# Three buffers instead of two for the gate and up weights of a mixture-of-experts stage, with the loads issued further ahead

## What is computed

```python
D_MODEL, D_EXPERT, N_EXPERTS, TOP_K = 1024, 512, 32, 2
# each token goes to the 2 best of the 8 experts in its best group of 4
def expert_mlp(args):
    xb, e = args
    h = jax.nn.silu(xb @ w_gate[e]) * (xb @ w_up[e])
    return h @ w_down[e]
# y[token] += gate * expert_mlp(x[token]); then x = LayerNorm(alpha*x + y)
```

## Time and profile before

| | |
|---|---|
| median of three runs | 2394.74 us |
| the profiled execution's own time | 2395.6 us |
| its span, first to last instruction | 2393.7 us |
| TensorE matmuls busy | 2159.0 us, 90% of the span |
| VectorE / ScalarE / GpSimd busy | 638.6 / 334.2 / 336.1 us |
| chain that ended last | 81% TensorE, 7% VectorE, 2% DMA |
| mean DMA rate | 220 GB/s |

### The profile page before, as it was taken

One profiled execution on the slowest core, in us unless ns is written; L12 is line 12 of the kernel. 1 busy time (PEld: TensorE's weight loads), 2 busy tenths in 40 slices (PEclk: granted clock), 3 DMA queues, 4 the chain that ended last, 5 costly groups with the idle time before them and its releaser, 6 DMA issues.

```text
span 2393.7 us, 29459 instructions
## 1 busy us (share of the span) xinstructions
PE 2159.0 (90%) x9808; PEld 1417.0 (59%) x9808; DVE 638.6 (27%) x1255; ACT 334.2 (14%) x827; POOL 336.1 (14%) x440
## 2 busy tenths in 40 slices
PE   7999978887999999999589999888699999999994
PEld 5566644555666666666356665444476666666662
DVE  1212166562111111111422113656601111111115
ACT  2000023210111111111010001323011111111111
POOL 0100011111111111111221000121111111111113
PEclk8999999997999999999789999999899999999995
DMA  7401011146899999999351110213459999999963
GB/s 246 125 32 39 18 48 72 53 167 229 313 381 387 372 374 373 376 373 356 134 186 36 36 36 19 65 72 121 180 217 348 373 378 380 368 377 375 368 247 147
DMA packets 101804, 526.37 MB, mean 220 GB/s; under 512 B 16362, under 2 KB 25578, under 8 KB 84994
## 3 DMA queue, kind: packets, MB, share of 16 engines
q1 hardware_dynamic: 86882, 491.58, 53.2%
q0 software_dynamic: 14848, 33.85, 5.6%
HBM read 489.95 MB, written 58.27 MB: 229 GB/s over the span
## 4 chain that ended last, share of the span: by engine, by line
PE 81%; DVE 7%; issue 5%; DMA 2%; POOL 2%; SPq 2%; ACT 1%; DVEq 0%; POOLq 0%; ACTq 0%
PE ps L775 21%; PE ps L544 19%; PE ps L808 11%; PE ps L660 9%; PE ps L779 8%; PE ps L812 4%; PE ps L758 3%; PE ps L612 1%; DVE arena L1545 1%; POOL rstd L1614 1%; DVE arena L1435 1%; PE ps L670 1%; DMA arena<-in_w_in 1%; DVE arena L1217 1%; DVE stat L1538 1%
## 5 line engine op out<-in xcount | busy, mean ns | idle before, releaser
L544 PE MATMUL ps<-arena 128*128 128x344 f32 x1728 | 510.7, 457 | 7.3 <-DMA arena<-in_w_in 4.5
L775 PE MATMUL ps<-arena 128*128 128x256 f32 x2304 | 510.0, 382 | 2.5 <-DVE arena L1435 2.5
L775 PEld LDWEIGHTS ps<-arena 128*128 128x128 f32 x2304 | 438.0, 191 | 87.6 <-issue 28.9
L544 PEld LDWEIGHTS ps<-arena 128*128 128x128 f32 x1728 | 331.1, 192 | 181.5 <-issue 14.4
L808 PE MATMUL ps<-arena 128*128 128x512 f32 x576 | 255.8, 597 | 20.3 <-ACT arena L1003 19.1
L1446 DVE SCALAR_TENSOR_TENSOR arena<-ps,gates,arena 128x256 f32<-128x256 f32 (+1 forms) x128 | 61.5, 480 | 664.2 <-ACT arena L998 664.2
L660 PE MATMUL ps<-arena 128*128 128x512 f32 x512 | 225.6, 598 | 14.3 <-ACT arena L951 11.0
L1658 POOL DMA_INDIRECT ytok<-arena,scol x64 | 98.7, 1542 | 973.1 <-DVE arena L1459 566.1
L781 PE MATMUL ps<-arena 128*64 128x256 f32 x896 | 199.4, 381 | 0.0
L779 PE MATMUL ps<-arena 128*64 128x256 f32 x896 | 199.4, 381 | 0.0
L808 PEld LDWEIGHTS ps<-arena 128*128 128x128 f32 x576 | 106.5, 190 | 148.3 <-issue 122.1
(11 more groups left out here) (217 smaller groups left out, 1695.1 us busy)
## 6 DMA issues: line engine op xcount, KB each, us to landing
arena<-in_w_gate SPq DMA_DIRECT2D x64, 2048.0 KB
arena<-in_w_up SPq DMA_DIRECT2D x64, 2048.0 KB, 19.9
arena<-in_w_down SPq DMA_DIRECT2D x64, 2048.0 KB, 20.0
arena<-in_w_in SPq DMA_DIRECT2D x36, 512.0 KB, 3.3
arena<-out_y_all SPq DMA_DIRECT2D x16, 512.0 KB, 3.2
xs<-arena SPq DMA_DIRECT2D x16, 512.0 KB, 2.7
ytok<-arena SPq DMA_DIRECT2D x16, 512.0 KB, 3.5
arena<-ytok SPq DMA_DIRECT2D x16, 512.0 KB, 6.5
```

Of the source, the lines that this page charges most:

```text
L544: last = mm(ps[:, 3 * half + ch, 0:CH], wring[:, slot, k * P:(k + 1) * P], xT[:, k, ch * CH:(ch + 1) * CH], start=(k == 0), stop=(k == KD ...
L775: last = mm(ps[:, 2 + q, at_c:at_c + 256], xgT[:, slot, k], w[slot][:, k, cols], start=(k == 0), stop=(k == KD - 1))
```

## The change

`wg` and `wu` get a third slot, at 32336 and 36432 of the arena. `wd`, `xgT` and `xg` keep two. Expert n uses slot n % 3 for gate and up weights, and n % 2 for down weights. TensorE raises `gu_mm` by 6 instead of 4 at the start, so the wait in `gate_up_in`, whose text is unchanged, is now for the expert three before; the waits of ScalarE and VectorE on `gu_mm` are moved by the same 2. Since 14 pairs don't divide by 3, TensorE's loop becomes 4 rounds of 3 pairs, with 2 of the 14 pairs and the last pair written out behind it. SyncE's loop becomes 4 rounds of 6 experts, between 2 experts ahead of it and 4 behind. SyncE also waits for the last output projection (`wo_mm`) before `order_ready`, since the third slot lies on `wo`.

```diff
+TURNS3 = ((NE + 2) // 3, (NE + 1) // 3, NE // 3)
...
-        wg = (at(8256, KD, DE), at(0, KD, DE))
-        wu = (at(12352, KD, DE), at(4096, KD, DE))
+        wg = (at(8256, KD, DE), at(0, KD, DE), at(32336, KD, DE))
+        wu = (at(12352, KD, DE), at(4096, KD, DE), at(36432, KD, DE))
...
-                def ranked_in(n, slot, col):
-                    e = sp.value_load(order[0:1, ds(col, 1)], min_val=0, max_val=NE - 1)
-                    gate_up_in(n, slot, e)
-                    down_in(n, slot, e)
-
+                def ranked_expert(col):
+                    return sp.value_load(order[0:1, ds(col, 1)], min_val=0, max_val=NE - 1)
+
+                sp.wait_ge(s["wo_mm"], BASE + NT * (l + 1) + 2)
+                settle(sp, s["sp_passed"])
                 sp.wait_ge(s["order_ready"], BASE + l + 1)
                 settle(sp, s["sp_passed"])
-                with sp.Fori(0, NPAIR) as i:
-                    ranked_in(2 * i + 2, 0, i + FIRST)
-                    ranked_in(2 * i + 3, 1, i + WIDE)
-                for slot in range(2):
-                    ranked_in(NE - 2 + slot, slot, WIDE - 2 + slot)
+                e = ranked_expert(FIRST)
+                gate_up_in(2, 2, e)
+                down_in(2, 0, e)
+                e = ranked_expert(WIDE)
+                gate_up_in(3, 0, e)
+                down_in(3, 1, e)
+                with sp.Fori(0, 4) as i:
+                    for j in range(6):
+                        e = ranked_expert(3 * i + (FIRST + 1 + j // 2 if j % 2 == 0 else WIDE + 1 + j // 2))
+                        gate_up_in(6 * i + 4 + j, (j + 1) % 3, e)
+                        down_in(6 * i + 4 + j, j % 2, e)
+                for j in range(4):
+                    n = NE - 4 + j
+                    e = ranked_expert((WIDE - 3, NE - 1, WIDE - 2, WIDE - 1)[j])
+                    gate_up_in(n, n % 3, e)
+                    down_in(n, j % 2, e)
...
-            pe.sem_inc(s["gu_mm"], 4)
+            pe.sem_inc(s["gu_mm"], 6)
...
-                    pe.wait_ge(s[f"wg_in{slot}"], BASE + 16 * (NE // 2 * l + turn + 1))
-                    pe.wait_ge(s[f"wu_in{slot}"], BASE + 16 * (NE // 2 * l + turn + 1))
+                    pe.wait_ge(s[f"wg_in{slot3}"], BASE + 16 * (TURNS3[slot3] * l + turn3 + 1))
+                    pe.wait_ge(s[f"wu_in{slot3}"], BASE + 16 * (TURNS3[slot3] * l + turn3 + 1))
...
-                with pe.Fori(0, NPAIR) as i:
-                    pair(2 * i + 2, i + 1, HALF, True)
-                pair(NE - 2, NE // 2 - 1, P, False)
+                with pe.Fori(0, NPAIR // 3) as i:
+                    for j in range(0, 6, 2):
+                        pair(6 * i + 2 + j, 3 * i + 1 + j // 2, ((j + 2) % 3, j % 3),
+                             (2 * i + (j + 2) // 3, 2 * i + (j + 3) // 3), HALF, True)
+                for j in range(0, 6, 2):
+                    e = NE - 6 + j
+                    pair(e, e // 2, (e % 3, (e + 1) % 3), (e // 3, (e + 1) // 3), HALF if j < 4 else P, j < 4)
...
-                    act.wait_ge(s["gu_mm"], BASE + 2 * n + 2)
+                    act.wait_ge(s["gu_mm"], BASE + 2 * n + 4)
```

More of the change, by code:

```diff
@@ L263, in build @@
             "ov_m", "ov_inv", "ov_idx",
-            "wg_in0", "wg_in1", "wu_in0", "wu_in1", "wd_in0", "wd_in1", "xg_in0", "xg_in1", "xg_mm",
+            "wg_in0", "wg_in1", "wg_in2", "wu_in0", "wu_in1", "wu_in2", "wd_in0", "wd_in1", "xg_in0", "xg_in1", "xg_mm",
             "xg_a", "xg_d", "gu_mm", "silu", "h_ready", "dn_mm", "y_a", "y_d", "sc_out0", "sc_out1", "ht_mm", "ht_a", "ht_d",
@@ L276, in build @@
                 "const_in", "copied", "ident_in", *(f"l2_in{t}" for t in range(NT)), "lnp_in", "ov_w", "small_out", "smp_in", "state_in", "w_in0",
-                "w_in1", "w_in2", "wd_in0", "wd_in1", "wg_in0", "wg_in1", "wo_in", "wu_in0", "wu_in1", "x1_out0",
+                "w_in1", "w_in2", "wd_in0", "wd_in1", "wg_in0", "wg_in1", "wg_in2", "wo_in", "wu_in0", "wu_in1", "wu_in2", "x1_out0",
                 "x1_out1", "x2_out", "xin0", "xin1", "xr_in0", "xr_in1"),
@@ L760, in gathered, with gate_up @@
                     last.then_inc(s["xg_mm"], 1)
-                def gate_up(e, slot, turn, rows):
+                def gate_up(e, slot, slot3, turn3, rows):
                     n = NE * l + e
@@ L774, in gate_up @@
                                 for k in range(KD):
-                                    last = mm(ps[:, 2 + q, at_c:at_c + 256], xgT[:, slot, k], w[slot][:, k, cols],
+                                    last = mm(ps[:, 2 + q, at_c:at_c + 256], xgT[:, slot, k], w[slot3][:, k, cols],
                                               start=(k == 0), stop=(k == KD - 1))
@@ L778, in gate_up @@
                             for k in range(KD):
-                                mm(ps[HALF:P, 2 + q, 0:256], xgT[:, slot, k, 0:HALF], wg[slot][:, k, cols],
+                                mm(ps[HALF:P, 2 + q, 0:256], xgT[:, slot, k, 0:HALF], wg[slot3][:, k, cols],
                                    start=(k == 0), stop=(k == KD - 1))
-                                last = mm(ps[0:HALF, 2 + q, 0:256], xgT[:, slot, k, 0:HALF], wu[slot][:, k, cols],
+                                last = mm(ps[0:HALF, 2 + q, 0:256], xgT[:, slot, k, 0:HALF], wu[slot3][:, k, cols],
                                           start=(k == 0), stop=(k == KD - 1))
@@ L816, in down, with pair @@
                     last.then_inc(s["dn_mm"], 1)
-                def pair(e, turn, second, then):
-                    gate_up(e, 0, turn, P)
+                def pair(e, turn, slot3, turn3, second, then):
+                    gate_up(e, 0, slot3[0], turn3[0], P)
                     gathered(e + 1, 1, turn, second)
@@ L822, in pair @@
                     down(e, 0, turn, P)
-                    gate_up(e + 1, 1, turn, second)
+                    gate_up(e + 1, 1, slot3[1], turn3[1], second)
                     if then:
@@ L829, in _ @@
                 gathered(0, 0, 0, P)
-                pair(0, 0, P, True)
+                pair(0, 0, (0, 1), (0, 0), P, True)
                 settle(pe, s["pe_passed"])
-                with pe.Fori(0, NPAIR) as i:
-                    pair(2 * i + 2, i + 1, HALF, True)
-                pair(NE - 2, NE // 2 - 1, P, False)
+                with pe.Fori(0, NPAIR // 3) as i:
[5 more added lines that the diff above has]
+                    pair(e, e // 2, (e % 3, (e + 1) % 3), (e // 3, (e + 1) // 3), HALF if j < 4 else P, j < 4)
                 settle(pe, s["pe_passed"])
@@ L994, in silu @@
                     for q in range(2):
-                        act.wait_ge(s["gu_mm"], BASE + 2 * n + q + 1 + 4)
+                        act.wait_ge(s["gu_mm"], BASE + 2 * n + q + 1 + 6)
                         act.wait_ge(s["h_ready"], BASE + 2 * n + q - 1)
@@ L1433, in xg_evict @@
                     dve.wait_ge(s["xg_mm"], BASE + n + 3)
-                    dve.wait_ge(s["gu_mm"], BASE + 2 * n + 2)
+                    dve.wait_ge(s["gu_mm"], BASE + 2 * n + 4)
                     v.tensor_copy(xgT[:, slot, 4:8, 0:rows], ps[:, 1, :].rearrange("p (k t) -> p k t", k=4)[:, :, 0:rows]
```

## The result

The changed kernel is slower: its runs gave 2408.15 to 2413.2 us, median 2412.35 (4 runs), against a median of 2394.3 of the kernel before in the same comparison. The ratio is 1.0073, with a 95% interval from 1.0056 to 1.0091. The forecast was 2402.0 us with a range up to 2412.0; the median lies 0.35 us above the end of that range, and the loss of 18 us is two and a half times the 7.3 us of the sum.

The account below looks back on a forecast made before the run. TensorE was taken as the bound, with the DMA queue close behind. Only the delayed first gathers cost time, 4.0 + 3.3 = 7.3 us, all other terms 0: 2402.0 us against the median of 2394.74, range up to 2412.

Parts of the forecast that it names:

- The steady loop: Loop of 14 pairs: the third slot removes no wait, since TensorE never waits for weights there; 0 us.
- theory G: Follow-up theory, not in the forecast: expert 2's 4 MiB load, issued just ahead of the first gather, slows that gather.
- the gather under load: Each layer's first gather, beside expert 2's early loads: 9.9 us instead of 5.94 and 6.58, adding 7.3 us; bound 12.7.
- other engines: Moved waits of ScalarE and VectorE are the same conditions, and SyncE's longer program delays nothing: 0 us.
- the length of TensorE's code: TensorE's loop body grows from one pair to three, 4.4 code packets instead of 1.5; taken as 0 us.
- Case A: Likeliest case: first gather of each layer delayed, all else hidden; 2402.0 us, own range 2395 to 2407.4; chance 57%.
- Rival C: TensorE's longer loop no longer stays resident, so each jump back needs a code fetch; some 2426 us; chance 15%.
- R: Follow-up theory, not in the forecast: a new register instruction lengthens the stretch before each full expert's down multiplication.
- The other sign: Second sign named for TensorE's loop code not staying resident: code packets in every round of the loop.
- Rival B: First gather of each layer lands as before, so the kernel is not slower: price 0, 2394.7 us; chance 22%.

Follow-up runs that it names:

- e6: Changed kernel with expert 2's gate and up loads issued after the first gather lands, and the down-weight wait behind the gate-and-up matmuls: 2394.08 us, ratio 1.0002.
- e1: Changed kernel, but SyncE issues expert 2's gate and up loads only after the layer's first gather has landed: 2403.94 us, ratio 1.0044.
- e9: Changed kernel, but only expert 2's gate weights (2 MiB) are issued before the first gather lands, the up weights after it: 2411.26 us, one execution.
- e7: Kernel before, with the waits for down weights and the last result's evictions moved out of down() to behind the gate-and-up matmuls: 2397.21 us, ratio 1.0017.
- e8: Kernel before, but all three loads of expert 1 are issued after the first gather has landed: 2392.5 us, ratio 0.9992.
- e10: Kernel before with expert 1's loads behind the first gather, and TensorE waiting for rk_done only behind the last expert: 2390.08 us, ratio 0.9981.
- e4: Kernel before, with only the down-weight semaphores and TensorE's waits on them 1 higher, so the value needs its own register instruction: 2401.83 us, ratio 1.0037.
- e5: Changed kernel, but the wait for the down weights stands behind the gate-and-up matmuls, before the transposes: 2405.45 us, ratio 1.0053.

## Why the prediction was right and wrong

**Right.** The steady loop gains nothing from the third slot: no weight wait was there, and e6 shows the slot by itself at 1.0002. The gate load of expert 2 is issued at 548.68 us, 0.16 us before the gather at 548.84, and the gather, named as the place of the loss, is where more than half of it lies. That is theory G, shown by e1. The issue and the first transposes (548.68 and 560.05 us, forecast about 552 and 563) came some 3 us early, since the stretch before them was shorter in this execution.

**A size was off: the gather under load.** The step took 9.9 us, the median of the gathers in the loop; it measured 10.97 and 11.41. The sum had 4.0 + 3.3 = 7.3 us for it, and it is 5.03 + 4.83 = 9.9, within the bound of 12.7. The prediction named a bias to the other side, that those 26 gathers run behind a scatter; why this one is slower still, no run tells.

**Not a term of the sum: the first gate-and-up.** It took 16.79 and 16.60 us in the two layers, instead of 16.10 and 15.76: 1.5 us more in all. Its length goes with the granted clock, which is the share of full speed: 0.50, its lower level, in the 9 us or so of waiting ahead of it, and 1.00 from 6 us behind its start. In its first 6 us it was 0.65 and 0.71 in the kernel before, 0.54 and 0.57 in the changed one. Behind gathers of 10 to 12 us it took 16.36 to 16.84 us in seven of eight cases (15.59 in e9), behind gathers of about 6 us 15.49 to 16.10 in eleven of twelve (17.01 in e7). But in e8 and e10, with the shortest gathers, it took 16.31 to 16.84 in all four. So the gather's length doesn't set it by itself, and whether the 1.5 us belong to the change stays open.

**The step that failed: "other engines" and the loop.** The prediction went through the moved waits of ScalarE and VectorE ("the same conditions: 0") and through the length of TensorE's code, but not through what the new wait values cost TensorE. It forecast the full gate-and-ups "still 36.22 us apart"; they are 36.46. The register instruction, and the waits that it pushes behind the end of the last eviction, cost 0.25 us per pair, and 32 pairs make it 8.0 us, which stood in the sum as 0. e4 shows it in the old kernel (7.1 us), and in e5 it is gone. The sum is now 9.9 + 8.0 = 17.9 us, against 18 between the medians (13 to 22 by the interval).

**What was luck.** That the measured time lies only 0.35 us above the range is not the sum's merit. Case A by itself ended at 2407.4; the range went up to 2412 as a margin for rivals of another kind, and the 8 us of the loop filled it.

**Rival C, the code that doesn't stay, fell,** and its sign was badly chosen: a period other than 36.22 us was to be C, and it was R. The other sign was right. In the changed kernel's DMA view from 722 to 1050 us, three rounds of the new loop with two of its three jumps back (827.8 and 937.2), there are two queues and none of them is code:

```profile
q1 hardware_dynamic: 14593, 112.86, 86.3%
q0 software_dynamic: 4032, 9.53, 11.4%
```

The 12 more code packets of the whole program (52 for 40) are fetched when the longer straight code is passed: 4 come from 612 to 722 us, the loop's first round among it, none from 722 to 1050 (nor from 716 to 724, around the first jump back at 718.4), and 7 from 1050 to 1170, where the loop is left. The kernel before has 4 from 603 to 1170. The Trainium skill's rule of a two-page window ("Runtime: NRT & Kernel Launch", Instruction fetch mechanics) would have a fetch at each jump of this loop, whose body is 4.4 packets long; the trace doesn't agree. The 128 KiB that the same section gives for TensorE are compatible with it: at 0.85 MB for 52 packets the body is, by estimate, some 72 KB.

**Rival B, the gather lands as before,** fell with the gathers themselves, 10.97 and 11.41 us.

## What to carry to other kernels

A prefetch that is issued earlier is not free even when it is early enough not to be waited for: look which small transfer on the critical path it now runs beside, and issue it behind that one. A change of buffer counts also changes the values that engines wait for; where a value was shared between semaphores, look at the instruction list for a new register instruction between an eviction and the matmul that waits for it, and move such a wait to where the engine has work queued. What costs is whatever stands behind the wait that ends last, here about 0.1 us for each instruction; waits that are long satisfied cost nothing ahead of it. Before adding a buffer, read whether anything waits for what it holds.

## What the runs showed that was not expected

One register instruction, with the wait that it pushes behind the last eviction's end, costs 0.25 us per use on TensorE, and nothing if it stands behind the gate-and-up matmuls (e5). No engine's busy time shows it. What stays open is why the compiler groups the waits as it does, and why the wait on `ht_d` alone (e7) ends 0.05 us later than the same wait grouped with one that was long satisfied.

A gather of 128 rows took 3.75 us (4.58 in the second layer) with no weight load beside it (e10), 5.94 with a tail of weight loads, 10.13 with 2 MiB and 10.97 with 4 MiB of them behind that tail. It nearly trebles. These are first-layer figures of one execution each. That the DMA engines are full to its end is shown for the 4 MiB (the view of the changed kernel above).
